# Experts' outputs added to the tokens on chip by TensorE, in place of a scatter to HBM and a read back

## The reference

```
for each token: group = argmax of 4; two experts of the 8 in that group; weights c1, c2
h_e   = silu(x @ wg[e]) * (x @ wu[e])          e = 0..31, wg, wu: 1024 x 512
out  += c * (h_e @ wd[e])                      wd: 512 x 1024
y     = RMSNorm(h + out) * final_g
```

## Time and profile before

| | |
|---|---|
| median of 3 runs | 1277.29 us |
| span of the profiled execution | 1275.0 us |
| PE busy | 1181.5 us (93% of the span) |
| PEld (weight loads) busy | 855.6 us |
| DVE, ACT, POOL busy | 450.1, 322.2, 93.7 us |
| moved by DMA | 283.18 MB, mean 222 GB/s |
| mean granted clock of TensorE | 0.976 |

### The profile page before, as it was taken

The page is one execution under the profiler, slowest core; times in us unless marked ns, Lnnn a source line. Parts: engine busy times, 40 slices in busy tenths (PEclk is TensorE's granted clock), DMA queues, the critical chain, the costliest instruction groups (busy, mean ns, idle before and its releaser), DMA issues.

```text
span 1275.0 us, 22261 instructions
## 1 busy us (share of the span) xinstructions
PE 1181.5 (93%) x9758; PEld 855.6 (67%) x9758; DVE 450.1 (35%) x804; ACT 322.2 (25%) x560; POOL 93.7 (7%) x132
## 2 busy tenths in 40 slices
PE   8999899999999999999999998999788888878895
PEld 8899888988898799999998784333233333323331
DVE  5347855553364453332333152121111111111116
ACT  5454343344315452322323141000000000000003
POOL 3100000001000100000000002111111111111100
PEclk9989999999999999999999999999999998999998
DMA  8210102302314822332336387999999999999995
GB/s 243 67 33 1 35 5 69 103 3 72 132 57 129 254 84 75 87 88 75 83 108 235 133 328 303 419 418 418 420 419 420 419 419 419 420 420 418 419 420 213
DMA packets 113420, 283.18 MB, mean 222 GB/s; under 512 B 23780, under 2 KB 71094, under 8 KB 88747
## 3 DMA queue, kind: packets, MB, share of 16 engines
q1 hardware_dynamic: 107546, 269.93, 55.8%
q0 software_dynamic: 5120, 9.46, 2.0%
q10 hardware_dynamic: 656, 2.36, 0.5%
HBM read 273.44 MB, written 15.60 MB: 227 GB/s over the span
## 4 chain that ended last, share of the span: by engine, by line
PE 68%; DMA 18%; DVE 6%; SPq 5%; ACT 1%; issue 1%; DVEq 0%; ACTq 0%
DMA slot<-in_e_wu_dram 18%; PE bank L667 8%; PE bank L1448 8%; PE bank L1386 6%; PE bank L1388 6%; PE bank L1387 6%; SPq L616 5%; PE bank L674 4%; PE bank L1508 2%; PE bank L1510 2%; PE bank L1509 2%; PE bank L1667 1%; PE bank L1621 1%; PE bank L1678 1%; PE bank L1560 1%
## 5 line engine op out<-in xcount | busy, mean ns | idle before, releaser
L667 PE MATMUL bank<-slot,xs 128*64 128x512 f32 x512 | 246.7, 632 | 62.5 <-DMA slot<-in_e_wu_dram 61.4
L668 PE MATMUL bank<-slot,xs 128*64 128x512 f32 x512 | 247.9, 634 | 0.0
L667 PEld LDWEIGHTS bank<-slot,xs 128*64 128x64 f32 x512 | 69.4, 144 | 204.4 <-issue 200.0
L1022 DVE TENSOR_TENSOR xs<-bank,g2x 128x512 f32<-128x512 f32 x32 | 22.1, 691 | 315.9 <-PE bank L791 315.9
L1386 PE MATMUL bank<-xnh,wh 128*128 128x256 f32 (+1 forms) x448 | 133.1, 297 | 0.6 <-DVE mt L3011 0.6
L1388 PE MATMUL bank<-xnh,low 128*128 128x256 f32 (+1 forms) x448 | 132.6, 296 | 0.0
L1387 PE MATMUL bank<-xnl,wh 128*128 128x256 f32 (+1 forms) x448 | 132.6, 296 | 0.0
L893 ACT ACTIVATE sg<-bank 64x512 f32<-64x512 f32 x32 | 19.0, 594 | 444.4 <-PE bank L668 444.4
L2563 DVE TENSOR_TENSOR low<-ring,wh 128x1536 fp32r<-128x1536 f32 (+1 forms) x45 | 89.9, 2005 | 79.6 <-ACT wh L2203 72.1
L674 PE MATMUL bank<-slot,ht 128*64 128x512 f32 x512 | 116.9, 598 | 0.5 <-DVE ht L1050 0.5
L1386 PEld LDWEIGHTS bank<-xnh,wh 128*128 128x128 f32 x448 | 85.0, 190 | 1.3 <-issue 1.2
(11 more groups left out here) (520 smaller groups left out, 2105.9 us busy)
## 6 DMA issues: line engine op xcount, KB each, us to landing
slot<-in_e_wg_dram SPq DMA_DIRECT2D x64, 1024.0 KB, 27.7
slot<-in_e_wu_dram SPq DMA_DIRECT2D x64, 1024.0 KB, 27.9
slot<-in_e_wd_dram SPq DMA_DIRECT2D x64, 1024.0 KB, 28.3
ring<-in_w_in_dram SPq DMA_DIRECT2D x13, 1024.0 KB, 5.2
ring<-in_w_in_dram SPq DMA_DIRECT2D x24, 512.0 KB, 4.3
ring<-in_w_branch_dram SPq DMA_DIRECT2D x24, 256.0 KB, 4.7
kvs<-in_cache_mem_k_dram SPq DMA_DIRECT2D x8, 512.0 KB, 5.6
kvs<-in_cache_mem_v_dram SPq DMA_DIRECT2D x8, 512.0 KB, 5.4
```

The lines of the kernel that those rows point to most:

```text
L667: pe.matmul(out[64:128, :], tok, wg[:, FF * k:FF * k + FF], start=(k == 0), stop=(k == KD - 1))
L668: mm = pe.matmul(out[0:64, :], tok, wu[:, FF * k:FF * k + FF], start=(k == 0), stop=(k == KD - 1))
```

## The change

No output of an expert goes to HBM. The block of each expert is kept in SBUF, scaled by the weight of each slot's pair (`cs`) and split in two fp32r parts, `yh` (written by ACT) and `yl`, the rest (written by DVE). DVE builds for each expert a matrix `wse` of 0 and 1, slots by tokens, by comparing two rows of token codes (`vsel`) with the code of each slot (`pcode`), in two instructions over 576 columns. TensorE multiplies `wse` with `yh` and `yl` for the five token tiles of expert `e - 2` between the steps of `gate_up(e)`, and DVE adds each product from PSUM to `h` in SBUF. PSUM banks are dealt out anew: gate and up have one bank, the output of `down` one, the products four (two pairs). The gathers of all experts are issued one after another; the scatters, their clearing and the reading back are gone from the path that is taken.

```diff
         def moe_sp(sp):
...
-            dve_t.wait(sp, "weights")
+            pe_t.wait(sp, "weights")
...
-            for t, (t0, tn) in enumerate(TILES):
-                for k in range(2):
-                    sp.dma_start(yb[t][0:tn, D * k:D * k + D], y_d.rearrange("(n k) d -> n k d", k=2)[t0:t0 + tn, k, :])\
-                        .then_inc(yb_loaded[t][k], 16)
...
         def moe_pe(pe):
...
-            dve_t.wait(pe, "weights")
+            dve_t.wait(pe, "lists")
             for i in range(2):
                 for t, (_, tn) in enumerate(TILES):
...
-                    for p in (0, 64):
-                        mm = pe.matmul(to[p:p + 64, :], wcol[0:tn, 5 * i + t, :], ident[0:tn, 0:tn], start=True, stop=True)
+                    mm = pe.matmul(to, code12[0:tn, i, t:t + 1].to_broadcast([tn, 128]), ident[0:tn, 0:tn], start=True, stop=True)
+            pe_t.done(mm, "codes")
+            idle_products(pe, 7, 8)
+            dve_t.wait(pe, "cw")
+            cw = post[:, :, :, :].rearrange("p k t e -> p (k t) e")
+            for n in range(10):
+                tn = TILES[n % 5][1]
+                for p in (0, 64):
+                    mm = pe.matmul(psum[HT_BANK][p:p + 64, 0:EX], place1[0:tn, n, :], cw[0:tn, n, :], start=(n == 0), stop=(n == 9))
...
+            def mix(e, t, start, stop, bank):
+                t0, tn = TILES[t]
+                if t == 0:
+                    dve_e.wait(pe, ("wse", e))
+                    dve_e.wait(pe, ("yl", e))
+                    act_e.wait(pe, ("yh", e))
+                n = last_one(e)
+                for part, y in enumerate((yh[n], yl[n])):
+                    for c in range(2):
+                        mm = pe.matmul(psum[bank + c][0:tn, :], wse[n][64 * c:64 * c + 64, t0:t0 + tn], y[64 * c:64 * c + 64, :],
+                                       start=(start and part == 0), stop=(stop and part == 1), skip_group_check=True)
+                return mm
...
             def gate_up(e):
...
+                for k in range(KD):
+                    if k % 4 == 0:
+                        for n in range(2):
+                            pe.wait_ge(eslot_loaded[(3 * e + n) % NSLOT][k // 4], 16 * ((3 * e + n) // NSLOT + 1))
+                    mm = expert_in(pe, psum[0], xs[e % 2], slots[3 * e % NSLOT], slots[(3 * e + 1) % NSLOT], range(k, k + 1))
+                    if k % 4 == 3:
+                        pe_m.done(mm, ("gu" if k == 7 else "gh", e))
+                    if e >= 2 and 2 <= k <= 6:
+                        t = k - 2
+                        n = 5 * (e - 2) + t
+                        if n >= 2:
+                            pe.wait_ge(added, n - 1)
+                        mix(e - 2, t, True, True, MIX_BANK[n % 2]).then_inc(mixed, 1)
...
+            for t in range(2):
+                pe.wait_ge(added, LAST_MIX - 1 + t)
+                mix(EX - 2, t, True, False, TAIL_BANK[t])
+            down(EX - 1)
+            mix(EX - 2, 2, True, False, TAIL_BANK[2])
+            for t in range(5):
+                if t >= 3:
+                    pe.wait_ge(added, LAST_MIX + t - 2)
+                    mix(EX - 2, t, True, False, TAIL_BANK[t])
+                mix(EX - 1, t, False, True, TAIL_BANK[t]).then_inc(mixed, 1)
...
         def moe_act(act, seq):
...
+                if e:
+                    pe_m.wait(act, ("d", e - 1))
+                    if 2 <= e < EX:
+                        act.wait_ge(mixed, 5 * (e - 1))
+                    act_e.done(act.activation(yh[last_one(e - 1)][:, :], psum[Y_BANK][:, :], ACT.Copy, scale=cs[:, e - 1:e]), ("yh", e - 1))
...
         def moe_dve(dve, seq):
...
+            def select(e):
+                to = wse[last_one(e)]
+                if 1 <= e < EX - 1:
+                    dve.wait_ge(mixed, 5 * e)
+                seq(dve.tensor_scalar(to[:, :], vsel[:, 0, :], pcode[:, e:e + 1], None, ALU.is_equal))
+                dve_e.done(dve.scalar_tensor_tensor(to[:, :], vsel[:, 1, :], pcode[:, e:e + 1], to[:, :], ALU.is_equal, ALU.add), ("wse", e))
+
+            def add(n, t, bank):
+                tn = TILES[t][1]
+                dve.wait_ge(mixed, n + 1)
+                hv = h[0:tn, t, :].rearrange("p (c n) -> p c n", c=2)
+                dve.tensor_tensor(hv, hv, banks8[0:tn, bank:bank + 2, :], ALU.add).then_inc(added, 1)
...
+                if 2 <= e < EX:
+                    for t in range(5):
+                        n = 5 * (e - 2) + t
...
+                        add(n, t, MIX_BANK[n % 2])
...
         def moe_pool(pool, seq):
...
-            for e in range(EX - 2):
-                if e + 3 < EX:
-                    gather(e + 3)
-                dve_e.wait(pool, ("y", e))
-                pool.indirect_dma_start(y_rows, bass.IndirectOffsetOnAxis(il[:, 1, e:e + 1].bitcast(U32), 0), yo[e % 2][:, :], None,
-                                        bounds_check=4 * NT - 1, oob_is_err=False).then_inc(scattered[e % 2], 16)
+            for e in range(EX):
+                gather(e)
```

More of the change, by code:

```diff
@@ L588, in build @@
         dve_o = Steps(sem("dve_o"), ["wr"] + [x for c in range(OUTS) for x in [("h", c, t) for t in range(5)] + ([("lg", c)] if c < OUTS - 1 else [])])
[L589 to L594, removed]
+        pe_t = Steps(sem("pe_t"), ["pos", "lists", "codes", "weights"])
+        mixed, added = sem("mixed"), sem("added")
+        LAST_MIX = 5 * (EX - 2)
+        act_t = Steps(sem("act_t"), ["root"] + [("x2", t) for t in range(5)] + ["exp_g", "exp_e", "codes"])
+        dve_t = Steps(sem("dve_t"), ["clear", "sumsq", "ms", "rstd", "lg", "dg", "sel", "places", "rows", "code", "lists", "addr", "de", "c12", "cw"])
+        dve_l = Steps(sem("dve_l"), ["zeros", "even", "gather0", "scatter0", "gather", "scatter"] + [("more", t, k) for t in range(5) for k in range(2)])
         pool_t = Steps(sem("pool_t"), ["far", "rows", "xg"])
@@ L794, in gate_up @@
             def gate_up(e):
                 dve_e.wait(pe, ("xs", e))
[L796 to L802, removed]
+                if e >= 1:
+                    dve_e.wait(pe, ("h", e - 1))
@@ L819, in turn_h @@
                 for f in range(4):
-                    mm = pe.transpose(psum[3][:, CAP * f:CAP * f + CAP], h2[:, 256 * (f // 2) + f % 2:256 * (f // 2) + 256:2], ident[0:CAP, 0:CAP])
+                    mm = pe.transpose(psum[HT_BANK][:, CAP * f:CAP * f + CAP], h2[:, 256 * (f // 2) + f % 2:256 * (f // 2) + 256:2], ident[0:CAP, 0:CAP])
                 pe_m.done(mm, ("ht", e))
[L823 to L835, removed]
-            turn_in(0)
[L838 to L844, removed]
+            turn_in(0)
+            for e in range(EX):
+                gate_up(e)
                 if e + 1 < EX:
@@ L1061, in final @@
                                                     ALU.mult, ALU.mult), ("y", t))
-            def pair(t):
-                tn = TILES[t][1]
-                act_f.wait(dve, ("scaled", t))
-                dve.wait_ge(yb_loaded[t][1], 16)
-                dve_f.done(dve.scalar_tensor_tensor(yb[t][0:tn, 0:D], yb[t][0:tn, D:2 * D], c12[0:tn, 1, t:t + 1], yb[t][0:tn, 0:D],
-                                                    ALU.mult, ALU.add), ("pair", t))
-            dve.wait_ge(fg_loaded, 16)
-            for t, (_, tn) in enumerate(TILES):
-                pair(t)
-                dve_f.wait(dve, ("pair", t))
-                pe_y.wait(dve, ("mix", t))
-                for c in range(2):
-                    cols = slice(512 * c, 512 * c + 512)
-                    last = dve.tensor_tensor(h[0:tn, t, cols], psum[MIX_BANK[t][c]][0:tn, :], yb[t][0:tn, cols], ALU.add)
-                dve_f.done(last, ("sum", t))
-                if t >= 1:
-                    final(t - 1)
-            final(4)
+            for t in range(5):
+                final(t)
         def moe_pool(pool, seq):
@@ L1090, in moe_pool @@
             pool.wait_ge(unit_used, len(units))
[L1091 to L1093 removed]
+            pool.iota(pcode_i[:, :], [[1, EX]], base=0, channel_multiplier=EX)
+            for k in range(2):
+                last = pool.iota(row_i[:, k, :], [[256, 5]], base=2, channel_multiplier=2)
             pool_t.done(last, "rows")
@@ L1136, in general_sp @@
             with sp.If(some_overflow(sp)):
-                pe_m.wait(sp, ("d", EX - 1))
+                dve_l.wait(sp, "zeros")
+                for n in range(2 * NT // 128):
+                    sp.dma_start(y_d[128 * n:128 * n + 128, :], zeros).then_inc(zeroed, 16)
                 sp.wait_ge(listed, 160)
@@ L1200, in general_dve @@
                         dve_n.done(dve.tensor_copy(yg[:, :], psum[4][:, :]), "y")
+                dve.wait_ge(yb_loaded, 16 * 5)
+                for t, (_, tn) in enumerate(TILES):
+                    for k in range(2):
+                        if k:
+                            dve_l.wait(dve, ("more", t, 0))
+                        dve_l.done(dve.scalar_tensor_tensor(h[0:tn, t, :], yb[t][0:tn, D * k:D * k + D], c12[0:tn, k, t:t + 1], h[0:tn, t, :],
```

(4 more changed lines are left out.)

191 lines of the change are left out of this document (81 added, 110 removed).

## The result

The changed kernel takes 1302.1 us (median of four runs, 1299.5 to 1303.2) against 1276.8 us of the kernel before beside it (1275.3 to 1279.3): 1.0195 times as long (95% interval 1.018 to 1.021). The forecast was 1300 us, slower. The profiled execution has a span of 1297.7 us and is the shortest of the four; the other spans are 1301.4, 1301.0 and 1299.7.

What follows compares the result with a forecast made beforehand. PE, at 15.80 us a turn, would replace the DMA (15.4) as bound: 799.1 + 29 turns gives 1257.3, last `gate_up` ends 1268.1, plus 29.2 is 1297.3 us span, median about 1300; range 1257 to 1325 us.

Steps and rivals of the forecast that it cites:

- The bound: Expert loop: PE's turn 11.90 us, DMA's 15.4 without scatters; over about 2.9 us more per turn lengthens the loop.
- The product: In `gate_up`: each of five products per turn costs PE 0.79 us, the fifth 0.05 less, 3.90 per turn.
- stream: In each product: two fp32r pairs, two matmuls side by side, at 0.23 us a pair.
- visit: In each product: fixed price of going to another tile shape, 0.19 us, and back to the gate matmuls, 0.14 us.
- The rest of the loop: DVE, ACT, SP and POOL work in the expert loop: hidden; DVE near 10 us of a 15.8 us turn.
- Routing: PE's work before the loop: first `gate_up` 0.5 us later, ends -1 and +3; third `gate_up` at 799.1 us.
- The end: From the last `gate_up`'s end to the kernel's end: 29.2 us against 36.1 before, 6.9 us won.
- 1 (free products, 1259 us): Expert loop: products nearly free at 0.46 us each, DMA stays the bound, median 1259 us; chance 0.15.
- 2 (a shorter stream): Products in `gate_up`: fp32r pair under 0.23 us, five products 3.0 us, 1273 us in all; chance 0.08.
- 3 (halves in turn): Products in `gate_up`: the array's row halves take turns in fp32r, 6.2 us per turn, 1369 us; chance 0.06.
- 4 (low clock in the loop): Expert loop: shape changes taken for idleness, mean clock 0.95, 23 us on top, 1323 us; chance 0.09.
- The sum: Whole kernel: third `gate_up`, 29 turns of 15.80 us, last `gate_up` and end give span 1297.3 us, median 1299.6.

Runs made afterwards that it cites:

- e7: Kernel before plus five idle f32 products per `gate_up` of experts 2 to 30, in the gate matmuls' tile shape: 1279.1 us, ratio 1.0018.
- e1: Changed kernel with the same five products per `gate_up` placed in three visits rather than five: 1281.7 us, 1.0041 of the kernel before.
- e4: Kernel before plus five idle products of the new shape, on constant data, in each `gate_up` of experts 2 to 30: 1306.4 us, ratio 1.024.
- e2: Changed kernel without the products and additions of experts 0 to 29, so their output is missing: 1254.1 us, 0.9837 of the kernel before.
- e3: Changed kernel without the `yl` matmuls for experts 0 to 29: 1265.7 us, 0.9915 of the kernel before.
- e8: Changed kernel, two experts' products in every second `gate_up`, three visits, the last behind its final step: 1263.4 us, 0.9891 of the kernel before.
- e5: Changed kernel with two experts' products added up in PSUM in every second `gate_up`, five visits, half the additions: 1276.7 us, 0.9997 of the kernel before.
- e6: Changed kernel with two experts' products in every second `gate_up`, in three visits, half the additions: 1264.8 us, 0.9900 of the kernel before.

## Why the prediction was right

**The bound.** The forecast rested on two paces, 11.90 us of PE and 15.4 of the DMA, and on the limit of about 2.9 us per turn beyond which a change lengthens the old loop. The experiments bracket it: +2.16 (e7) costs 0.2%, +3.31 (e1, with the shorter end already in it) 0.4%, and +4.0 (changed, e4) 2 to 2.4%. e2 shows the DMA's pace without the scatters at 15.4, as forecast; against that faster DMA the limit is the 2.5 us above, which the prediction did not work out.

**The product.** Forecast 0.79 us = 0.46 stream + 0.33 visit, measured 0.81. The stream is confirmed by e3 (0.234 per pair), the visit by e1 (0.345). The error of 0.02 us a product is 29 x 0.10 = 2.9 us in the sum. The two parts of the visit hold as well: the 0.11 and 0.09 behind `yh` and `yl` are 0.20 (forecast 0.19, from `mix_y`), the 0.10 and 0.05 at the gate pairs 0.15 (forecast 0.14, from `gate_up`). The pairs run side by side: each row x2 of line 803 holds two matmuls and the next starts 0.23 us on.

**The rest of the loop.** Costed at nothing, with VectorE as cover: its additions took 1.22 us each (mean of 155), and by its list of waits PE waited for none of them before the tail; e4, which has none, has the same turn. This row of the costliest groups (count, then busy and mean ns, then the idle time before and its cause) shows that the additions wait for PE:

```profile
L1026 DVE TENSOR_TENSOR h<-h,bank 128x1024 f32<-128x1024 f32 (+1 forms) x155 | 188.8, 1220 | 119.0 <-PE bank L803 119.0
```

**Routing.** Forecast 799.1 for the third `gate_up`, in the trace 795.43, which is 3.7 us early. The idle products began at 762.57 rather than 765.99, 3.4 us early by themselves, and the work ahead of them, which the change does not touch, ran up to there at a mean clock of 1.00 rather than 0.99 (stretches at half clock of 6.8 us in all, against 17.1). From their start to the third `gate_up` it was 32.86 us against 32.65 before, so the edit itself cost 0.2 us (forecast 0.5). The rest is luck: in the eight traces of the experiments, which leave the work up to there as it was, the third `gate_up` begins anywhere from 795.5 to 802.7 us. The other three runs of the changed kernel, 2.0 to 3.7 us longer in span, have no trace; that they lacked this luck is likely and not shown.

**The end.** Forecast 29.2 us from the end of the last `gate_up`, measured 1297.7 - 1267.38 = 30.3. The rows are PE's there: `down` of expert 31 has the same 16 records as that of expert 30, but took 5.35 us and not 3.60.

```profile
1267.38 3.60 PE L668 MATMUL bank<-slot,ht 128*64 128x512 f32 x16
...
1272.77 0.50 PE L803 MATMUL bank<-yh,wse 64*128 64x512 f32 x2 [1.16 <-DVE yl L1047]
...
1273.89 5.35 PE L668 MATMUL bank<-slot,ht 128*64 128x512 f32 x16
1279.17 0.50 PE L803 MATMUL bank<-yh,wse 64*128 64x512 f32 x2
```

The row of busy time over that `down` has a mean granted clock of 0.68, so part of it ran at 1.2 GHz:

```profile
1273.89:1279.17 5.28, 5.28 (x18) 1.44 (x16) 0.23 (x1) 0.00 (x0) 0.00 (x0) 0.68 0.00 0
```

PE had paused for 1.16 us just before, but that alone does not explain it: in e8 PE paused as long at the same place, and the same `down` stayed at 1.00 and took 3.6 us. There the end was 1261.6 - 1232.94 = 28.7 us, and it was 28.5 to 28.7 in the traces of e1, e2, e3, e5 and e6 too. What lowered the clock in this one execution stays open. The term of the end was thus 0.5 us too high by its own steps, and a low clock that I had not counted, which six other traces do not have, put 1.7 on it.

**The rivals.** 1 (free products, 1259 us) fell: no wait for weights is left, and e2's 1254 shows what its world looks like. 2 (a shorter stream) fell by the 0.234 us of e3. "TensorE: Matmul & The Clock Gate" of the Trainium skill gives about 131 ns per matmul of 512 columns in its section Back-to-back issue gap, which the rival took for a pair side by side. The runs do not bear that out: the pair takes 0.23 us, and so does a single fp32r matmul over the whole array. 3 (halves in turn) fell by the distance of 0.23 us. 4 (low clock in the loop) fell by 1.00 in both stretches.

**The sum.** 1297.3 was forecast for the span. Against it stand -3.7 (routing and the luck ahead of it), +2.9 (turns), +0.1 (the last `gate_up`) and +1.1 (the end): 1297.7. The errors cancel in this one execution; against the median of 1302.1 the forecast of 1300 is 0.2% low, about what the turns were short of. That the span came out within half a microsecond is luck; that the turn, the product and the DMA's pace did is not.

## What to carry to other kernels

Tile shape here means how the array is divided into rows and columns for a matmul. Between matmuls of one tile shape a few of another cost more than their columns: here 0.35 us per visit out and back, 43% of a product's 0.81 us. Before such work goes into a stream, gather it: the same arithmetic in 1.5 visits per expert rather than 5 turned +25 us into -13 (in e8, where VectorE also adds half as often; e4 shows that its additions were not what cost). And compare added work with the slack per turn over the whole loop, buffers that are full at its start included: up to that limit it is nearly free, behind it each 0.1 us per product costs 15 us.

## What the runs showed of the hardware that I had not expected

In the kernel before the granted clock was 0.95 from 868 to 1232 us. In e7 it was 1.00 there, and the time was no shorter: its later turns were 15.9 us, against 15.8 before. The low clock fell on a PE that waited for the DMA, and cost nothing that the runs show. The prediction names 18 us of it among what goes with the change; its sum does not use them, since they lay inside the wait.

```profile
868.00:1232.00 364.00, 344.65 (x1828) 149.85 (x1829) 55.90 (x98) 14.26 (x24) 48.57 (x48) 1.00 1.02 419
```

It is tempting to say that e7 kept the full clock because PE was busier, 345 us of the 364 rather than 302. e2 speaks against it: there PE was busy for 281 of 346 us, a smaller share than before, with 67.4 us of waits for weights against 61.4, and the clock was 1.00 as well. What lowered it in the kernel before stays open.

```profile
868.00:1214.00 346.00, 280.83 (x1288) 107.17 (x1284) 82.94 (x139) 29.47 (x46) 26.27 (x21) 1.00 1.01 419
```
